# First weight parts of the retention values: two raw places and another order of use; one long tile moved between the value tiles

## The reference

```python
h = rmsnorm(x, g_pre) * (1.0 + scale) + shift
proj = h @ w_in            # latents, gates, retention q, k, v
y_mla = mla_branch(...)    # q and k from low-rank latents, rotary, causal attention, 8 heads
y_ret = retention_branch(q_ret, k_ret, v_ret, ...)   # rotary, 4 heads, chunks of 128 tokens
merged = sigmoid(merge_mla) * (y_mla @ w_proj_mla) + sigmoid(merge_ret) * (y_ret @ w_proj_ret)
out = rmsnorm(x + gate * (merged @ w_out), g_final)  # gate: a row from silu(c) @ w_ada
```

## Time and profile before

| | |
|---|---|
| median of 3 runs | 1690.85 us |
| the profiled execution | 1690.0 us, its span 1688.2 us |
| PE busy | 1609.5 us, 95% of the span |
| mean granted TensorE clock | 0.98 |
| DVE, ACT, POOL busy | 56%, 34%, 13% |

### The profile page before, as it was taken

One profiled execution on the slowest core, in us unless ns is written; L12 is line 12 of the kernel. 1 busy time (PEld: TensorE's weight loads), 2 busy tenths in 40 slices (PEclk: granted clock), 3 DMA queues, 4 the chain that ended last, 5 costly groups with the idle time before them and its releaser, 6 DMA issues.

```text
span 1688.2 us, 20245 instructions
## 1 busy us (share of the span) xinstructions
PE 1609.5 (95%) x7780; PEld 1344.8 (80%) x7780; DVE 946.4 (56%) x1467; ACT 581.3 (34%) x1005; POOL 212.9 (13%) x157
## 2 busy tenths in 40 slices
PE   4999999999999899897999999799899999999998
PEld 4778888888888788785888888688688887888886
DVE  6984444444448666457455565455566666545543
ACT  5443333333342222422343343334334334212211
POOL 2232322223201221013000000000000000000000
PEclk8999999999999999899999999899899999999999
DMA  9033233223332757879655464536988887523322
GB/s 385 21 125 113 107 109 121 107 109 110 121 122 66 228 215 283 317 245 299 228 182 198 162 225 162 194 128 218 403 281 271 263 266 234 187 99 137 131 91 84
DMA packets 164848, 310.16 MB, mean 184 GB/s; under 512 B 11024, under 2 KB 104080, under 8 KB 156816
## 3 DMA queue, kind: packets, MB, share of 16 engines
q1 hardware_dynamic: 152800, 274.45, 46.7%
q0 software_dynamic: 5760, 20.97, 3.2%
q10 hardware_dynamic: 6192, 13.44, 2.5%
HBM read 196.62 MB, written 111.67 MB: 183 GB/s over the span
## 4 chain that ended last, share of the span: by engine, by line
PE 76%; DVE 10%; DMA 7%; issue 2%; POOL 2%; ACT 2%; SPq 1%; ACTq 0%; DVEq 0%; POOLq 0%
PE p_banks L1935 9%; PE p_banks L1893 8%; PE p_banks L1895 8%; PE p_banks L1896 8%; PE p_banks L1966 5%; PE p_banks L2140 3%; PE p_banks L2139 3%; PE p_banks L2138 3%; PE p_banks L1804 2%; PE p_banks L1806 2%; PE p_banks L1805 2%; PE p_banks L2037 2%; PE p_banks L2188 2%; PE p_banks L2187 2%; PE p_banks L2186 2%
## 5 line engine op out<-in xcount | busy, mean ns | idle before, releaser
L489 ACT ACTIVATE w_hi<-w_raw 128x1024 fp32r<-128x1024 f32 (+3 forms) x81 | 72.2, 893 | 230.0 <-PE p_banks L2140 103.8
L1431 DVE TENSOR_TENSOR w_form<-w_pair,w_form 128x512 fp32r<-128x512 f32 x120 | 92.9, 776 | 102.0 <-ACT w_form L1098 100.8
L1098 ACT ACTIVATE w_form<-w_pair 128x512 fp32r<-128x512 f32 x120 | 75.6, 632 | 195.1 <-PE p_banks L1896 187.1
L1804 PE MATMUL p_banks<-h_hi,w_hi 128*128 128x512 f32 x304 | 119.7, 394 | 2.7 <-DVE w_lo L495 2.7
L1806 PE MATMUL p_banks<-h_hi,w_lo 128*128 128x512 f32 x304 | 118.4, 390 | 0.0
L1805 PE MATMUL p_banks<-h_lo,w_hi 128*128 128x512 f32 x304 | 118.4, 390 | 0.0
L495 DVE TENSOR_TENSOR w_lo<-w_raw,w_hi 128x1024 fp32r<-128x1024 f32 (+2 forms) x82 | 95.9, 1170 | 33.0 <-ACT w_hi L489 32.9
L2140 PE MATMUL p_banks<-y_hi,w_lo 128*128 128x512 f32 x256 | 99.7, 389 | 0.0
L2138 PE MATMUL p_banks<-y_hi,w_hi 128*128 128x512 f32 x256 | 99.7, 389 | 0.0
L2139 PE MATMUL p_banks<-y_lo,w_hi 128*128 128x512 f32 x256 | 99.7, 389 | 0.0
L1893 PE MATMUL p_banks<-h_hi,w_form 128*128 128x512 f32 x240 | 93.6, 390 | 1.1 <-DVE w_form L1431 1.1
(11 more groups left out here) (273 smaller groups left out, 4280.9 us busy)
## 6 DMA issues: line engine op xcount, KB each, us to landing
w_raw<-in_w_dense SPq DMA_DIRECT2D x45, 512.0 KB, 5.1
w_pair<-in_w_pairs SPq DMA_DIRECT2D x20, 1024.0 KB, 4.8
qk_chunk<-qk_chunks SPq DMA_DIRECT2D x32, 640.0 KB, 4.8
qk_chunks<-split_stage SPq DMA_DIRECT2D x32, 512.0 KB, 5.9
v_ret<-v_stage POOLq DMA_DIRECT2D x32, 512.0 KB, 3.9
v_chunk<-v_ret SPq DMA_DIRECT2D x32, 512.0 KB, 5.4
merge_t<-act_t SPq DMA_DIRECT2D x48, 256.0 KB, 3.2
act_t<-stage SPq DMA_DIRECT2D x40, 256.0 KB, 2.0
```

The costliest lines, as they stand in the source:

```text
L1431: nc.vector.tensor_tensor(self.form[f % FORM_SLOTS][:, 1, :], self.form_source(f), self.form[f % FORM_SLOTS][:, 0, :].bitcast(F32), ALU.su ...
L1804: nc.tensor.matmul(out, w_hi[:, slot, cut], x_hi[:, k, tok], start=(k == ks[0]), stop=False)
```

## The change

The tile x10 is moved from behind v3 to behind v1: k4 v0 k5 v1 x10 k6 v2 k7 v3 x11 ... x15. `R_GATE_ROW`, the place behind the last `v` tile, is now x11: POOL's loads of the gate's rows stand at x11 to x14, at x11 and x13 behind the rotation adds in POOL's order, and DVE's steps stay at x11 to x14. The first value weights get a second raw place, `v_raw`, for parts 1 and 3: part 1 is loaded together with part 0, part 2 when part 0 is lowered, part 3 when part 1 is lowered. Part 3 is copied by ACT and lowered by DVE inside the turn of x15, ahead of that turn's rotation splits. In the first pair of units the parts 0, 1 and 2 are used for both units (36 products) and then part 3 for both (12).

```diff
 for n in range(4):
     SEQ += [("k", 4 + n), ("v", n)]
-SEQ += [("x", n) for n in range(10, TURNS)]
+    if n == 1:
+        SEQ += [("x", 10)]
+SEQ += [("x", n) for n in range(11, TURNS)]
...
+        self.v_raw = at("v_weight_raw_aside", Z + 32 * KB, [P, D])
...
     def raw_place(self, r):
+        if r in (R_V + 1, R_V + 3):
+            return self.v_raw[:, :]
...
     def load_weight(self, queue, r):
-        if R_V <= r <= R_MERGE + 1:
+        if r in (R_V + 1, R_V + 2, R_V + 3):
+            if r > R_V + 1:
+                queue.wait_ge(self.w_lo_ready, r - 1)
+        elif R_V <= r <= R_MERGE + 1:
             queue.wait_ge(self.w_lo_ready, r if r <= R_MERGE else R_MERGE)
...
     def fill_product(self, m):
         pair, m = divmod(m, 2 * UNIT)
-        if pair and pair % 4 in (0, 3):
+        if not pair:
+            ahead = 2 * (UNIT - 6)
+            late = m >= ahead
+            half, m = divmod(m - ahead, 6) if late else divmod(m, UNIT - 6)
+            return half, m // 3 + (KD - 2 if late else 0), m % 3
+        if pair % 4 in (0, 3):
...
     def sync(self, sp):
...
-                ahead = [s for s in range(self.split_total) if s >= self.splits[R_GATE_ROW + 1]]
+                ahead = [s for s in range(self.split_total) if s >= self.splits[R_GATE_ROW]]
...
     def scalar(self, act):
...
             elif r + RING >= R_V:
-                self.load_weight(act, r + RING)
+                self.load_weight(act, r + RING + (r + RING > R_V))
+                if r + RING == R_V:
+                    self.load_weight(act, R_V + 1)
...
             self.split_weight(act, r + RING)
+            if r == R_V - 1:
+                self.split_weight(act, R_V + RING)
...
-        self.load_weight(act, R_V + RING)
         self.scalar_attention(act)
...
     def vector(self, dve):
...
             self.lower_weight(dve, r + RING)
+            if r == R_V - 1:
+                self.lower_weight(dve, R_V + RING)
...
-            if 0 <= r - R_GATE_ROW - 1 < KD // 2:
-                for k in range(2 * (r - R_GATE_ROW - 1), 2 * (r - R_GATE_ROW)):
+            if 0 <= r - R_GATE_ROW < KD // 2:
+                for k in range(2 * (r - R_GATE_ROW), 2 * (r - R_GATE_ROW + 1)):
```

More of the change, by code:

```diff
@@ L532, in fill_unit_end @@
         pair, half = divmod(unit, 2)
-        return 2 * UNIT * pair + (UNIT * (half + 1) if pair % 4 in (1, 2) or not pair else 2 * UNIT - 6 * (1 - half))
+        return 2 * UNIT * pair + (UNIT * (half + 1) if pair % 4 in (1, 2) else 2 * UNIT - 6 * (1 - half))
     def filled_by(self, step):
@@ L1146, in scalar_attention @@
         units = parts = 0
-        self.split_weight(act, R_V + RING)
         for g in range(STEPS + 4):
@@ L1533, in vector_attention @@
         units = parts = 0
-        self.lower_weight(dve, R_V + RING)
         for g in range(STEPS + 4):
```

## The result

Before: 1690.95 us (median of 17 runs, 1687.59 to 1693.39). After: 1695.68 us (median of 17, 1692.17 to 1697.72). The ratio is 1.0028, 95% interval 1.0022 to 1.0035: 4.7 us slower. The profiled execution of after took 1696.5 us with a span of 1694.7, against 1690.0 and 1688.2. The forecast was 1689.7; the time lies inside the range of 1684.5 to 1696, at its far end, on rival B's 1695.7.

A forecast was written before the change was run, and what follows sets the result against it. PE, busy 95% of the span, was taken as the bound. Terms of -3.4 (x10's move), -0.3 (second scores) and +2.5 us (low clock) summed to -1.2, on the median 1690.85 giving 1689.7 us; range 1684.5 to 1696.

The forecast's parts named there:

- rival B: Slower: late gate loads and steps delay x15's splits and stores, second scores at 817; +4.8 us, 1695.7 us; chance 0.20.
- Part 1: x10 behind v1: the stop in v3 and its low clock go, the v1 stop grows slightly; -3.4 us.
- Part 2: Gate's rows: last step ends near 789.6 instead of 785.2, PE's stop grows from 1.8 to about 6 us; alone costs nothing.
- The stores' row: DVE's wait for the stores until 756.62, ahead of x12's rotation, moves 1 to 2.5 us with 1 MB more.
- Part 4: Second scores wait for exponentials behind x15's stores, landing 809.5, scores at 811.3; of 9.85 + 2.6 us gives back -0.3.
- Part 3: Value weights: part 3 ready near 797, so the 9.85 us stop and its 2.6 us clock loss go.
- Part 5: Low clock behind PE's new idle time before the second scores; +2.5 us (0.5 to 4).
- A: Stores keep up in idle DMA shares, last lands at 807.5, second scores at 809.3; -4.7, 1686.1 us; chance 0.22.
- C: The stop is simply gone, second scores do not wait for the stores; -14.7, 1676 us; chance 0.05.
- D: The stop in v3 stays, k6's store landing late behind x10's traffic; +2.2, 1693 us; chance 0.08.

The follow-up runs named there:

- move alone: Kernel before with x10 moved behind v1 only, gate loads in their old order against the adds, value weights as before: 1687.44 us, 0.9983.
- 5: Kernel after with POOL's third pair of gate loads ahead of x13's adds, only the first pair still behind x11's adds: 1689.51 us, 0.9993.
- 6: Kernel after with POOL's first pair of gate loads ahead of x11's adds, only the third pair still behind x13's adds: 1688.99 us, 0.9988.
- experiment 1: Kernel after with POOL's eight gate loads one turn earlier, at v3, x11, x12, x13: 1685.44 us, 0.9972.
- Experiment 8: Kernel after with six of POOL's eight gate loads left out, the two loaded row blocks used for all eight steps: 1684.47 us, 0.9966.
- experiment 3: Kernel before with the value weights' part of the change only, x10 and gate loads left in place: 1688.7 us, 0.9989.
- 7: Kernel after without the value weights' part: x10 moved, POOL's gate loads late at x11 to x14: 1693.77 us, 1.0016.
- experiment 4: Kernel before with POOL's eight gate loads one turn later, at x11 to x14, and nothing else changed: 1698.78 us, 1.0047.

## Why the prediction went wrong, by its steps

**Part 1 was right.** The stop in v3 is gone; the one in v1 grew from 6.2 to 6.9 us, the upper end of 0 to 0.7. Gain 3.1 us against 3.4, and 2.7 in the median of the move alone. One profile can't tell 3.1 from 3.4, since x11's row scatters by 1.9 us.

**Part 2 is the step that failed, in its sizes.** Its direction, the order of the loads and who waits behind whom all came as written. Three terms were too small, and one assumption fell. The last gate step ended at 795.1 in before's times instead of 789.6, and of these 5.5 us 3.3 came by the issue of loads 4 and 5 (774.9 instead of 771.6), 1.4 by their landing and 0.8 by loads 6 and 7.

- The stores' row was to move 1 to 2.5 us; it moved from 756.62 to 761.9 in before's times, 5.2 us. I counted 1 MB at 429 GB/s, 2.4 us. But the moved loads were not the only ones to get ahead of the store's landing. In before loads 2 and 3 left just behind the store (750.38 and 751.78) and most of their bytes moved after it had landed; in after steps 0 and 1, which I called free because DVE idles there, let them go at 749.53 and 751.91, and the store, held up by loads 0 and 1, was still under way. So 1.57 MB more of gate rows moved between its issue and its landing (1.96 against 0.39), and 0.73 MB more of stores. Each gate load took 1.57 us of the engines instead of 1.2 (four took 34.8% of 18.1 us, 6.3 us). Experiments 5 and 6 show this row alone: 758.85 and 752.76.
- Loads 4 and 5 were to land in 4.6 us; they took 5.5 and 6.9. The 4.6 us were the best row of before, for a load that left in an emptier place; I wrote "at best" and then used it as the value.
- Loads 6 and 7 were taken at 8 to 9; they took 6.9 and 9.8 (issues at 778.90 and 780.86, steps at 785.80 and 790.70).
- Together they make PE's stop at the gate row 11.7 us instead of 6.
- The assumption, from Part 4 and rival B: up to 791 the stores would wait for DMA anyway, so a chain that ends sooner costs nothing. The traces show no such point. Below stand the end of the last gate step and the start of ACT's table load, which waits for the last store's landing, each in its own kernel's times:

```
kernel                         last gate step ends   landing   between
1  after, loads early                 778.93          800.76     21.8
8  after, two gate loads              779.53          801.14     21.6
2  move alone                         780.24          802.95     22.7
3  weights alone                      784.67          806.34     21.7
   before                             785.23          807.53     22.3
6  third pair late                    785.46          806.16     20.7
5  first pair late                    787.40          808.06     20.7
7  move, loads late                   790.70          810.73     20.0
   after                              791.98          812.67     20.7
4  before, loads late                 796.74          816.79     20.1
```

The landing follows the last step at 20.0 to 22.7 us over 18 us of delay. It goes nearly one for one even where the step ends earlier than before's. A common delay of everything in DVE's order would look the same, but experiment 4 moves nothing but the loads, and there +11.5 us at the step bring +9.3 at the landing; in 5 and 6 against 1, +8.5 and +6.5 bring +7.3 and +5.4. Experiment 8 is no exception: without six of the loads its last step ends no earlier than in experiment 1, and x15's rotation could hardly start earlier either, since it waits for PE's own products of x15 until 779.71. SP's queue hid only 2 to 3 us of a later chain. In before SP issued x15's last two stores 5.5 us behind the end of DVE's splits (794.50, 799.98), in after 1.3 us behind it (802.25, 803.57); but from issue to the table load it then took 9.1 us instead of 7.6. So the landing I took at 809.5 came at 815.8 in before's times; 5.5 of these 6.3 us are those of the last gate step.

**Part 3 was right.** No wait for the fourth part; its load, issued at 784.00, landed 8.6 us later, in time. The two subtractions took 2.47 and 3.42 us, together 5.8 from start to end, where I had 4 to 5. Yet the added one cost x15's splits only 1.0 us, near the 1.2 taken: they end 10.3 us behind the last gate step in after, 9.3 in before and in experiments 4 and 7. The wait for POOL's second add, which the added subtraction now carries, stood in the splits themselves before (4.54 us for the two, 2.35 in after). Their rows and POOL's show a turn-taking: POOL's add from 793.21 ends at 795.56, the subtraction that began at 794.17 ends 1.08 us later; POOL's second add takes 3.37 us instead of 2.35 and ends at 798.89, and the second subtraction ends 1.09 us behind it. The Trainium skill, "SBUF — State Buffer", section "SBUF: two separate sides", says that a DVE operation with two SBUF inputs and a GpSimd operation lock each other out for a whole instruction. The trace agrees: each subtraction needs its 1.1 us after the add has ended.

**Part 4 was right in kind, not in size.** PE did reach the second scores and stand there, waiting for ACT, and ACT for a store out of `split_stage`. The stop was 6.8 us (foreseen 3 to 7), but from 817.6 in before's times and not from 811.3; that is the 6.3 us that Part 2 lost. The premise behind the landing, that DMA is full from 770 on so that the stores move by the bytes ahead of them, did not hold in after. There the engines had idle time to spare while loads 4 and 5 stood behind POOL's adds and DVE waited for them; before at 770 to 785 us, then after in the same stretch of before's times:

```profile
770.00:785.00 15.00, 13.50 (x60) 10.86 (x58) 10.20 (x9) 1.97 (x3) 1.09 (x2) 1.00 0.96 295
...
766.90:781.90 15.00, 13.49 (x60) 10.85 (x58) 11.07 (x8) 3.12 (x4) 6.99 (x6) 1.00 0.63 188
```

What moved the landing was the chain, load after step after load. The bytes count where they hold up one of its links, as they did with the store ahead of x12's rotation.

**Part 5 was right.** 2.8 us lost behind the second scores against 2.5.

The sum by the measured terms: -3.1 for Part 1, +6.0 for the second scores (817.6 - 811.62), +2.8 for the clock, +5.7 in the profile. Rival B had written -3.4 + 5.2 + 3 = +4.8; the median moved +4.7. B's mechanism is what the runs show, with one difference: it needs no threshold. That its number fits to 0.1 us is in part luck: it took 9 us for each of loads 4 to 7, which took 5.5, 6.9, 6.9 and 9.8, and it had none of what the first pair did to x12's row beyond Part 2's 1 to 2.5 us. Rivals A and C are out by the rows at 812.67 and 814.47, D by the stop in v3 that went. I gave B 0.20 because loads 4 and 5 left "at the edge of the empty stretch"; the chain of eight loads should have been stepped through with the landing times of a full stretch, as B did to reach 794, and with the two loads that its first steps let go.

## What to carry to other kernels

Ask of a moved load not only when its own data are needed but what stands ahead of it in its engine's queue and which in-order queue waits for it; two pairs of loads that slipped behind 5.8 us of adds each, with the two other pairs a turn later, cost 8.6 us of the kernel with the same work (experiment 4). Price a load, above all the one that lets the next ones go, with the landing time of a full stretch, and count as well the store that lands behind it. When a stop is taken away, follow the release behind it, and the one behind that: with `prob` apart a stop of the same length came up 27 us further on, and one load's place in SP's order then gave 0.45% at once.

## What the runs showed of the hardware that I had not expected

- A store of 512 KB landed in 12.6 us while 1.96 MB of gate loads moved, and in 7.3 us while 0.39 MB of them did. Each gate load of 512 KB took 1.57 us of all 16 engines (34.8% of 18.1 us for four); the stores' queue took 48.2% for 2.62 MB, 1.74 us for the same bytes. A full stretch thus held 0.5 MB per 1.6 to 1.7 us, not the 1.2 that the best stretch of before gave.
- Stops of 6.8 to 7.1 us ahead of the second scores were followed by low clock over 5.0 to 5.6 us of PE's work each time: 5.63 busy in after (814.4 to 820.1 at 0.50), 5.03 in experiment 1 (800.7 to 807.6 at 0.51), 5.15 in experiment 3 (803.0 to 813.3 at 0.50). Half of the busy time is lost: 2.5 to 2.8 us, about the same for all three.
